# A depthwise convolution on four engines: GpSimd's partial sums enter TensorE's bank through an identity matmul, and VectorE adds one bank per block, two blocks later

## The reference, cut to what matters

```python
def conformer_conv(x, w_pw1, b_pw1, w_dw, b_dw, ln_g, ln_b, w_pw2, b_pw2):
    u = x @ w_pw1 + b_pw1
    u = u[..., :D_MODEL] * jax.nn.sigmoid(u[..., D_MODEL:])
    u = lax.conv_general_dilated(          # depthwise, causal, CONV_WIDTH = 31 taps
        u, w_dw[:, None, :].astype(u.dtype), window_strides=(1,),
        padding=[(CONV_WIDTH - 1, 0)], dimension_numbers=('NWC', 'WIO', 'NWC'),
        feature_group_count=D_MODEL) + b_dw
    uf = u.astype(jnp.float32)
    m = jnp.mean(uf, axis=-1, keepdims=True)
    var = jnp.mean(jnp.square(uf - m), axis=-1, keepdims=True)
    u = ((uf - m) * lax.rsqrt(var + CONV_LN_EPS) * ln_g + ln_b)
    return jax.nn.silu(u) @ w_pw2 + b_pw2
```

## Time and profile before

| | us |
|---|---|
| median of three runs | 1275.65 (1272.88 to 1276.87) |
| the profiled execution, its own time | 1274.57 |
| its span | 1272.8 |
| TensorE busy | 1142.5 (90% of the span) |
| VectorE busy | 527.0 (41%) |
| ScalarE busy | 402.8 (32%) |
| GpSimd busy | 217.5 (17%) |
| the convolution, from the first gate (804.0) to the end of `finish(7)` (924.8) | 120.8 |

### The profile page before, as it was taken

How to read it: one execution, slowest core, us unless ns; L and a number is a source line. 1 busy time by engine, 2 the same in 40 slices (tenths; PEclk the granted TensorE clock), 3 DMA queues, 4 the chain that set the end, 5 groups by cost and what they waited for, 6 DMA issues and landing times.

```text
span 1272.8 us, 29413 instructions
## 1 busy us (share of the span) xinstructions
PE 1142.5 (90%) x12654; PEld 614.9 (48%) x12654; DVE 527.0 (41%) x931; ACT 402.8 (32%) x782; POOL 217.5 (17%) x228
## 2 busy tenths in 40 slices
PE   4999999999999989899988886999999899987780
PEld 2355555555555644455544433444544455544440
DVE  6855554553555412411111105799942511111115
ACT  3335435444344321311111113455443311111112
POOL 2000000000000002122211110588701122211110
PEclk9999999999999989999999998999999999999996
DMA  5011101011012156699999987126301799999985
GB/s 171 3 53 61 32 27 51 11 54 40 19 57 83 58 211 252 252 409 423 423 424 427 426 353 271 67 68 257 153 1 39 281 405 424 424 425 426 426 338 223
DMA packets 50209, 271.95 MB, mean 214 GB/s; under 512 B 16386, under 2 KB 19586, under 8 KB 31648
## 3 DMA queue, kind: packets, MB, share of 16 engines
q1 hardware_dynamic: 38048, 240.67, 47.0%
q0 software_dynamic: 10880, 21.00, 4.4%
q10 hardware_dynamic: 1152, 8.39, 1.6%
HBM read 263.73 MB, written 23.07 MB: 225 GB/s over the span
## 4 chain that ended last, share of the span: by engine, by line
PE 58%; DMA 21%; DVE 14%; ACT 3%; issue 2%; SPq 2%; POOLq 0%; DVEq 0%; ACTq 0%
DMA big<-in_moe_w_gate_up_dram 16%; PE psum L1269 14%; PE psum L841 10%; PE psum L1770 9%; PE psum L1431 6%; DVE psum L2173 6%; PE psum L854 4%; DMA conv_w<-in_moe_w_gate_up_dram 3%; DVE h L944 2%; PE psum L1548 1%; PE psum L820 1%; PE psum L1572 1%; PE psum L1420 1%; PE psum L2026 1%; DVE big L435 1%
## 5 line engine op out<-in xcount | busy, mean ns | idle before, releaser
L841 PE MATMUL psum<-big 128*64 128x256 f32 x1728 | 217.9, 396 | 41.4 <-DMA big<-in_moe_w_gate_up_dram 30.2
L1269 PE MATMUL psum<-big 128*128 128x512 f32 x384 | 192.6, 622 | 4.7 <-ACT big L1303 3.1
L841 PEld LDWEIGHTS psum<-big 128*64 128x64 f32 x1728 | 120.7, 141 | 124.2 <-DMA big<-in_moe_w_gate_up_dram 42.1
L915 DVE TENSOR_TENSOR big<-big,psum 128x128 f32<-128x128 f32 x64 | 18.4, 288 | 325.2 <-ACT big L882 325.2
L781 POOL DMA_INDIRECT chosen<-big x64 | 63.7, 995 | 347.1 <-ACT big L892 179.4
L854 PE MATMUL psum<-big 128*64 128x512 f32 x512 | 120.8, 593 | 1.2 <-ACT big L887 1.2
L1770 PE MATMUL psum<-big 128*128 128x512 f32 x256 | 114.7, 600 | 0.8 <-ACT big L2126 0.8
L2026 PE MATMUL psum<-big,conv_w 128*128 128x512 f32 x256 | 110.3, 593 | 1.2 <-ACT big L415 1.2
L1613 ACT COPY big<-psum 128x512 f32<-128x512 f32 (+1 forms) x112 | 68.5, 649 | 117.5 <-PE psum L1431 115.6
L754 POOL TENSOR_SCALAR big<-big 128x1024 f32<-128x1024 f32 x4 | 11.4, 2854 | 544.0 <-PE psum L462 543.9
L1998 POOL TENSOR_TENSOR big<-big 128x512 f32<-128x512 f32 x74 | 96.0, 1297 | 44.0 <-ACT big L2108 34.0
(11 more groups left out here) (256 smaller groups left out, 1307.2 us busy)
## 6 DMA issues: line engine op xcount, KB each, us to landing
big<-in_moe_w_gate_up_dram SPq DMA_DIRECT2D x54, 2048.0 KB, 28.2
big<-in_moe_w_down_dram SPq DMA_DIRECT2D x64, 1024.0 KB, 33.6
conv_w<-in_moe_w_gate_up_dram SPq DMA_DIRECT2D x10, 2048.0 KB, 33.1
big<-in_rwkv_w_rkv_dram SPq DMA_DIRECT2D x24, 512.0 KB, 4.0
conv_w<-in_conv_w_pw_dram SPq DMA_DIRECT2D x8, 1024.0 KB, 4.8
big<-chosen ACTq DMA_DIRECT2D x8, 1024.0 KB, 7.8
big<-in_rwkv_w_o_dram SPq DMA_DIRECT2D x4, 1024.0 KB, 9.2
rows<-big POOLq DMA_DIRECT2D x8, 512.0 KB, 6.6
```

Of the source, the lines that this page charges most:

```text
L841: last = nc.tensor.matmul(o[half * SLOTS:(half + 1) * SLOTS, 0:F_EXP].rearrange("p (u f) -> p u f", u=2), m.xT[e // 2 % 2][:, c, (e % 2) * ...
L1269: last = nc.tensor.matmul(bank[b], m.w[:, n, c, :], x[:, c, :], start=(c == 0), stop=(c == C - 1))
```

## The change

GpSimd's sum of a block no longer goes to VectorE. TensorE multiplies it by the identity, which adds it into the bank in which its own taps stand (bank 0 in blocks 0 to 4, which have no taps on TensorE; there the identity matmul starts the bank). VectorE's `finish(q)` then is one addition from that bank, and stands in the middle of block q + 2 instead of q + 1. GpSimd now reuses a `pooled` tile once TensorE has read it (`pe_tapped`), not once VectorE has.

```diff
@@ pool_conv @@
                 if q >= 2:
-                    pool.wait_ge(m.co_ready, q - 1)
+                    pool.wait_ge(m.pe_tapped, q - 1)
@@ pe_conv @@
                 for i in range(PE_TAPS[q]):
                     at = TAPS - PE_TAPS[q] + i
-                    last = nc.tensor.matmul(bank[TAP_BANK[q]], m.diagonal[first + i], m.u[b][:, at:at + T],
-                                            start=(i == 0), stop=(i == PE_TAPS[q] - 1))
-                last.then_inc(m.pe_tapped, 1)
+                    nc.tensor.matmul(bank[TAP_BANK[q]], m.diagonal[first + i], m.u[b][:, at:at + T],
+                                     start=(i == 0), stop=False)
+
+            def pooled(q):
+                pe.wait_ge(m.pooled_ready, q + 1)
+                if 1 <= q and not PE_TAPS[q]:
+                    pe.wait_ge(m.co_ready, q)
+                nc.tensor.matmul(bank[TAP_BANK[q]], ident[:], m.pooled[q % 2], start=not PE_TAPS[q],
+                                 stop=True).then_inc(m.pe_tapped, 1)
...
             for q in range(C - 1):
                 products(q)
+                if q >= 3:
+                    pooled(q - 3)
             taps(C - 3)
             products(C - 1)
+            pooled(C - 4)
             pe.wait_ge(m.mean_of_ready, 1)
             pe.wait_ge(m.w2_in, 16)
             pe.wait_ge(m.sig_ready, C - 1)
             taps(C - 2)
+            pooled(C - 3)
             for q in range(C - 3):
                 mean(q)
             taps(C - 1)
+            pooled(C - 2)
             mean(C - 3)
+            pooled(C - 1)
             mean(C - 2)
-            stay_busy(1)
             mean(C - 1)
             stay_busy(1)
@@ dve_conv @@
             def finish(q):
-                b, co = q % 2, m.co[:, q, :]
+                co = m.co[:, q, :]
                 dve.wait_ge(m.tap, summed[q])
-                dve.wait_ge(m.pooled_ready, q + 1)
-                last = nc.vector.tensor_tensor(co, m.pooled[b], co, ALU.add)
-                if PE_TAPS[q]:
-                    dve.wait_ge(m.tap, st.done(last))
-                    dve.wait_ge(m.pe_tapped, sum(1 for e in PE_TAPS[:q + 1] if e))
-                    last = nc.vector.tensor_tensor(co, bank[TAP_BANK[q]], co, ALU.add)
-                last.then_inc(m.co_ready, 1)
+                dve.wait_ge(m.pe_tapped, q + 1)
+                nc.vector.tensor_tensor(co, bank[TAP_BANK[q]], co, ALU.add).then_inc(m.co_ready, 1)
...
-                    if q and k == FINISH_AT:
-                        finish(q - 1)
+                    if q >= 2 and k == FINISH_AT:
+                        finish(q - 2)
...
+            finish(C - 2)
             finish(C - 1)
```

More of the change, by code:

```diff
@@ L1891, in bass_hybrid_rwkv7_conformer_hmoe @@
         POOL_TAPS = (11,) * 5 + (10, 9, 8)
-        TAP_BANK = {5: 1, 6: 2, 7: 4}
+        TAP_BANK = (0,) * 5 + (1, 2, 4)
         FINISH_AT = 8
```

## The result

| | before | with the change |
|---|---|---|
| median of four runs, us | 1276.26 (1272.88 to 1277.18) | 1283.80 (1282.80 to 1286.29) |
| profiled execution: its own time | 1274.57 | 1282.80 |
| its span | 1272.8 | 1281.0 |
| TensorE busy | 1142.5 | 1148.2 |
| VectorE busy | 527.0 | 519.9 |

The ratio of the times is 1.0058, 95% interval 1.0038 to 1.0077: the changed kernel is slower, by some 7 us. Forecast were 1282.0 and slower.

A forecast was written before the change was run, and what follows sets the result against it. The prediction took VectorE's work to bound the convolution stage, TensorE and GpSimd being near full; 1274.57 + 6.8 = 1281.4 us, or 1282.4 by the runs' median, so forecast 1282.0, range 1279 to 1286, let down to 1278.5.

The forecast's parts named there:

- VectorE's saving, 7.4 us: Convolution: old additions of 10.6 and 1.9 us give way to eight from a bank, 5.1; VectorE's work falls 7.4.
- TensorE's added work and where it reaches `pooled`: Eight matmuls of 0.86 us in TensorE's full, in-order queue; `pooled(0)` and `pooled(4)` late, VectorE waiting 5.9 and 4.1.
- GpSimd: right in time: GpSimd's block 6 waits for `pooled(4)`, starting at 908.0 instead of 897.62; additions 1.45 us apart end at 929.6.
- The end of the stage: After GpSimd's last addition, `pooled(7)` and the last means follow; `mean(7)` starts at 931.6 against 924.83, 6.8 us later.
- nothing is taken up behind the stage: Behind the convolution, centring, projection and SyncE's loads move with it, so the whole 6.8 us counts.
- This is the step that decides: Where TensorE reaches the `pooled` matmuls: done when its queue gets there, making VectorE wait 5.9 and 4.1 us.
- low bound, 4.7: End of the stage: with faster GpSimd additions, TensorE's own queue still makes it 4.7 us later.
- VectorE's saving goes through: Rival, chance 0.05: TensorE reaches `pooled(0)` by 839.4 and is as early at `pooled(4)`; stage shortens, 1268 us.
- The waits and the saving cancel: Rival, chance 0.06: TensorE rows take 0.41 us or less, GpSimd's block 6 starts before 903; about 1276 us.
- VectorE's account, waits less savings: Convolution stage: VectorE's waits 5.9 + 4.1 + 0.7 + 3.5 = 14.2 us against 7.4 of work saved.
- The clock rival: Rival, chance 0.04: TensorE's granted clock falls in the new waits, doubling the next 15 us; up to 1297 us.

The follow-up runs named there:

- e1: The changed kernel with each identity matmul one projection sooner in TensorE's queue; ratio to before 1.0036, stage 141.4 us.
- e2: The kernel before plus eight unread identity matmuls on TensorE in the change's places, without one `stay_busy`; ratio 1.0043, stage 141.1 us.
- e3: The changed kernel with three `pooled` tiles in turn instead of two; ratio 1.0031, stage 141.4 us.
- e4: e1 with new tap shares in blocks 5 to 7: TensorE 1, 5, 5, GpSimd 11, 10, 8, VectorE 19, 16, 18; ratio 0.9975, stage 134.0 us.
- e5: The changed kernel, identity matmuls late as in the change, with the tap shares of e4; ratio 1.0057, stage 143.8 us.
- e7: The kernel before with the tap shares of e4, without identity matmuls; ratio 1.0039, stage 142.4 us.
- e8: e5 with seven identity matmuls into a free bank just ahead of `pooled(7)`, filling TensorE's wait; ratio 1.0028, stage 141.5 us.

## Why the prediction was right, and where its reasons were not

- **VectorE's saving, 7.4 us: right.** It is 7.1 by busy time. The additions from a bank took 0.68 to 0.69 beside a working GpSimd, as the one row of before had it.
- **TensorE's added work and where it reaches `pooled`: right.** The rows stayed 0.43 apart; `pooled(4)` was through 117.7 + 0.86 after the first projection, as worked out. VectorE's waits were 5.76 and 4.11 for 5.9 and 4.1; the one at the gate of block 7 was 0.15 for 0.7, and those at the end were 0.67 + 3.19 = 3.9 for 3.5.
- **GpSimd: right in time, slightly off in two sizes that cancel.** Its block 6 began 118.8 after the first projection (forecast 118.9) and its last addition ended at 931.5, which is 929.4 on the clock of before (forecast 929.6). The additions were 1.42 apart and not 1.45, (14.03 - 1.28) / 9, and there were pauses of 0.45 and 0.24 between groups, which the sum did not have.
- **The end of the stage: 6.8 forecast, 6.7 measured.** The number was no luck: the sum for the end went by TensorE's queue and GpSimd's restart, which are the two that e1, e2 and e3 bear out. That nothing is taken up behind the stage fits, but is not shown: the 0.6 lies within the spread of that part.
- **"This is the step that decides" was wrong.** The prediction put the weight on VectorE's waits for `pooled(0)` and `pooled(4)`. e3 keeps both and e1 has neither, and their stages are the same 141.4. What decides is that TensorE had only 2.35 us to spare by the end and got 6.9 us of work (4.5 of the loss in e1 and e3, and 4.3 where e2 adds it alone), and that GpSimd restarts late (2.2, shown by e3). The prediction had the first only as a low bound, 4.7, "TensorE's own queue holds it even if GpSimd is faster".
- **Two rivals had wrong signs.** "VectorE's saving goes through" was to hold if TensorE reached `pooled(0)` by 839.4 and was as early at `pooled(4)`. In e1 it does both (on the clock of before `pooled(0)` starts at 830.4 and `pooled(4)` at 888.8), and the stage is 4.5 longer than before: the condition forgot the sum of TensorE's queue. "The waits and the saving cancel" named a pace of 0.41 per row, which was not met (0.43), and as its sign that GpSimd's block 6 starts before 903. In e3 it starts 110.3 after the first projection, 899.5 on the clock of before, and 4.5 are still lost: without the faster rows the sign means nothing. For a gain, two things were needed together, as in e4: TensorE gives work away, and the identity matmuls stand early. Either alone lost (e5 and e1). VectorE's account, waits less savings, gave the right sum all the same, because its last wait is by definition whatever TensorE is late by; such an account proves nothing about which wait matters.
- **The clock rival: not here, but near.** In the changed kernel the wait of 1.89 us left the granted clock at 1.00. In e5 and e7, with 7.27 and 6.76, it fell and cost 2.3 and 0.9 in the stage, and in e7 another 1.5 (3.47 - 1.95) between the first centring and the first variance.

## What to carry to other kernels

Before moving work onto an engine because another one is the bound, add up that engine's own queue to the point where the two meet: TensorE was off the critical path here with 2.35 us to spare, and 6.9 us of added matmuls turned it into the bound, whether they stood early (e1) or late (e2, e3). Long waits that a change creates on the old bound are then a symptom; to see whether they cost anything, remove them alone (a buffer more, an earlier place) and watch the end of the stage. And a relief of one engine is only worth something with a new share of the work: with the identity matmuls early the kernel is 0.36% slower with the old table of taps (e1) and 0.25% faster with a new one (e4). The order counts as well: with the new table and the matmuls late it is 0.57% slower (e5).

## What the runs showed that I had not expected

- TensorE's granted clock fell in the long waits and charged what followed. After waits of 7.27 and 6.76 us the next two rows of 128x512 and four of 128x256 took 2.08 and 2.07 us instead of 1.13; after 1.89 and 1.26 us they took 1.13. Seven idle matmuls in the wait paid for themselves (e8 against e5, -2.3 us in the stage). e7 has a case in between: behind 3.65 us of waiting, ten rows of `taps(7)` took 7.39 us, where ten rows took 4.46; its granted clock from 905 to 940 was 0.76. I made no run on that one.

```profile
913.91 7.39 PE L2036 MATMUL psum<-big 128*128 128x512 f32 x10 [3.65 <-DVE big L2140]
```

- GpSimd loses by VectorE's additions from SBUF too, but little: ten additions took 14.28 us with one such addition among them and 14.03 without, 0.25 less. VectorE's own additions had taken 1.04 to 1.55 us beside a working GpSimd and 0.70 without, so they lost 0.3 to 0.9. The Trainium skill (SBUF — State Buffer, Who interferes with whom) has it that the second of two such instructions waits until the first is through. The prediction had taken up to 0.7 per block from that and from VectorE's rows, as what GpSimd might get back; this case's trace says 0.25.
